# Four norms joined tile by tile with the stages around them

## What is computed

```python
# first block, end of the mixer, experts, final norm
h = h + g1 * (merged @ w_out)                     # mixer's out projection
x = modulate(rmsnorm(h, norm_ffn), sh2, sc2)      # "ffn" norm
h = h + g2 * hier_moe(x)                          # routed experts, 2 picks per token
h = rmsnorm(h, norm_final)                        # first final norm
# second block
hn = rms_norm(h, g_mix)                           # "mix2" norm
# ... latent and dilated attention on hn @ w_in ...
h = h + mixed @ w_out                             # attention's out projection
h = h + peer_ffn(rms_norm(h, g_ffn))              # "ffn2" norm, memory stage
gate = sigmoid(rms_norm(h, g_ple) @ w_ple_gate)   # "ple" norm, gate projection
h = h + gate * (p @ w_ple_proj)
return rms_norm(h, g_final)                       # last norm
```

## Time and profile before

| | us |
|---|---|
| runs of the kernel before | 3147.31, 3138.82, 3145.73 |
| their median | 3145.73 |
| profiled execution | 3139.65 |
| its span, first to last instruction | 3137.8 |
| TensorE busy, share | 2779.3, 89% |
| VectorE busy, share | 1446.8, 46% |
| ScalarE busy, share | 534.6, 17% |
| GpSimd busy, share | 748.5, 24% |

### The profile page before, as it was taken

The page is one execution under the profiler, slowest core; times in us unless marked ns, Lnnn a source line. Parts: engine busy times, 40 slices in busy tenths (PEclk is TensorE's granted clock), DMA queues, the critical chain, the costliest instruction groups (busy, mean ns, idle before and its releaser), DMA issues. The chain is left out here.

```text
span 3137.8 us, 28344 instructions
## 1 busy us (share of the span) xinstructions
PE 2779.3 (89%) x10072; PEld 1566.3 (50%) x10072; DVE 1446.8 (46%) x2990; ACT 534.6 (17%) x1149; POOL 748.5 (24%) x620
## 2 busy tenths in 40 slices
PE   6999999999997699949889989999866789888877
PEld 3446534456444333324445578888755633333333
DVE  1135200112011322231057249888789977777762
ACT  2024200011001011130147121111122400000011
POOL 0000000000000122110000004456588556555630
PEclk9999998999997799979899999999988999999998
DMA  5101241520123699841300028999999689999981
GB/s 206 54 27 56 108 188 61 221 91 34 54 107 135 242 420 391 340 185 54 115 14 1 27 89 310 408 389 394 374 331 369 218 347 413 413 412 413 413 352 74
DMA packets 142432, 694.17 MB, mean 221 GB/s; under 512 B 20451, under 2 KB 21859, under 8 KB 110563
## 3 DMA queue, kind: packets, MB, share of 16 engines
q1 hardware_dynamic: 59716, 408.31, 33.1%
q0 software_dynamic: 81792, 281.07, 23.1%
q10 hardware_dynamic: 800, 3.15, 0.3%
HBM read 701.89 MB, written 48.23 MB: 239 GB/s over the span
## 5 line engine op out<-in xcount | busy, mean ns | idle before, releaser
L2237 POOL DMA_INDIRECT wring<-in_peer_u,pm_rows x256 | 368.5, 1440 | 736.4 <-DVEq L2530 536.8
L2349 PE MATMUL ps<-hT 128*128 128x512 f32 x1024 | 462.5, 604 | 65.7 <-DVE hT L2554 43.8
L422 PE MATMUL ps<-hT,wring 128*128 128x512 f32 (+2 forms) x1232 | 467.8, 541 | 13.5 <-DMA pm_iota<-in_row_numbers 3.5
L422 PE MATMUL ps<-hT,pm_coef_table 128*128 128x256 f32 x2048 | 451.2, 382 | 0.0
L422 PEld LDWEIGHTS ps<-hT,pm_coef_table 128*128 128x128 f32 x2048 | 392.3, 193 | 53.6
L2560 DVE SCALAR_TENSOR_TENSOR h_tok<-wring,pm_coef,h_tok 128x1024 f32<-128x1024 f32 x256 | 325.0, 1282 | 119.0 <-DMA wring<-in_peer_v,pm_rows 117.4
L2237 POOL DMA_INDIRECT wring<-in_peer_v,pm_rows x256 | 314.0, 1227 | 248.6 <-DVE h_tok L2560 209.8
L2349 PEld LDWEIGHTS ps<-hT 128*128 128x128 f32 x1024 | 189.8, 191 | 337.8 <-issue 232.8
L422 PEld LDWEIGHTS ps<-hT,wring 128*128 128x128 f32 (+1 forms) x1232 | 233.6, 191 | 241.3 <-issue 232.8
L2439 DVE CUSTOM_DVE_ANT_0 wring<-wring,pm_coef_table 128x1024 f32<-128x1024 f32 x256 | 306.0, 1232 | 71.8 <-DMA wring<-in_peer_u,pm_rows 66.6
L1454 POOL COPY ex_idx<-row_token 128x1 uint32 (+1 forms) x24 | 4.5, 186 | 1174.4 <-PEq L1586 1043.7
(11 more groups left out here) (416 smaller groups left out, 2759.6 us busy)
## 6 DMA issues: line engine op xcount, KB each, us to landing
ex_gu<-in_experts SPq DMA_DIRECT2D x32, 2048.0 KB
pm_coef_table<-in_peer_uT SPq DMA_DIRECT2D x64, 1024.0 KB
hT<-in_peer_v SPq DMA_DIRECT2D x64, 1024.0 KB
ex_dn<-in_experts SPq DMA_DIRECT2D x48, 1024.0 KB
wring<-in_w_in SPq DMA_DIRECT2D x21, 2048.0 KB, 8.6
wring<-in_experts SPq DMA_DIRECT2D x16, 2048.0 KB
ada_w<-in_w_ada SPq DMA_DIRECT2D x12, 2048.0 KB
g_dram_out<-pm_coef_table SPq DMA_DIRECT2D x64, 256.0 KB
```

The costliest lines, as they stand in the source:

```text
L422: mm = env.nc.tensor.matmul(out, w[:, k, lo:hi], rhs(k), start=(k == 0), stop=(k == KD - 1))
L2237: nc.gpsimd.indirect_dma_start(ring[n % RING], None, dram[name], bass.IndirectOffsetOnAxis(ap=rows[:, t, j:j + 1], axis=0)).then_inc(got[n ...
L2349: mm = nc.tensor.matmul(env.ps[:, OUT[k], :], W[n % 2][:, at:at + P], vr[p % 2][:, m % 2 * D + k % 2 * WBLK:m % 2 * D + (k % 2 + 1) * WBLK ...
```

## The change

A class `TileNorm` does the same norm for one token tile at a time: ScalarE squares tile t and takes its root, VectorE takes the reciprocal and scales the tile, TensorE transposes its eight 128x128 blocks into two banks, ScalarE evicts the first bank and VectorE the second, in four instructions each of 128x128. It is woven into its neighbours:

- The mixer's out projection takes the token tile outermost and both weight blocks within, and its tiles go tile 0, tile 1, transposes of 0, tile 2, transposes of 1, and so on; the store of xn goes tile by tile.
- The expert sum has the first final norm and the "mix2" norm behind it in one stage. ScalarE evicts four of the eight p @ w_ple_proj products ahead of its first scaling, and the other four later. The row of gains is one more load in this stage, and the stage waits for its stores.
- The attention's out projection takes the token tile outermost, with the transposes of tile i-1 behind the products of tile i. Both weight blocks are now free only when the last tile is reached.
- The "ple" norm, the gate projection and the last norm are one stage: transposes of tiles 0 and 1, gate products of tile 0, transposes of 2 and 3, the other gate products; each tile is normed by row and stored as soon as its sum is complete. Square roots and sigmoids alternate on ScalarE.

Six stages with their barriers are gone: four `stage_norm` and two `stage_rownorm`.

```diff
+class TileNorm:
+    def rows_on_scalar(self, act, t):
+        nc.scalar.activation(self.xn[:, t, :], self.env.h[:, t, :], ACT.Square, accum_out=self.ss[:, t, :]).then_inc(self.sq_done, 1)
+        act.wait_ge(self.sq_done, self.sq0 + t + 1)
+        nc.scalar.activation(self.rs[:, t, :], self.ss[:, t, :], ACT.Sqrt, scale=1.0 / D,
+                             bias=self.env.eps[:, 0:1]).then_inc(self.rms_done, 1)
+    def rows_on_vector(self, v, t):
+        v.wait_ge(self.rms_done, self.r0 + t + 1)
+        nc.vector.reciprocal(self.ss[:, t, :], self.rs[:, t, :]).then_inc(self.inv_done, 1)
+        v.wait_ge(self.inv_done, self.i0 + t + 1)
+        nc.vector.tensor_scalar(self.xn[:, t, :], self.env.h[:, t, :], self.ss[:, t, :], None, ALU.mult).then_inc(self.done, 1)
+    def on_tensor(self, pe, t):
+        pe.wait_ge(self.done, self.done0 + t + 1)
+        for half, tl in enumerate(self.tiles[t]):
+            bank_ready(env, pe, tl)
+            for j in range(4):
+                mm = nc.tensor.transpose(env.ps[:, tl[0], j * P:(j + 1) * P],
+                                         self.xn[:, t, (4 * half + j) * P:(4 * half + j + 1) * P], env.ident[:])
+            mm.then_inc(env.bank_full[tl[0]], 1)
+    def columns_on_scalar(self, act, t):
+        product_done(env, act, tl)
+        for j in range(4):
...
+    def columns_on_vector(self, v, t):
+        product_done(env, v, tl)
+        for j in range(4, KD):
...
@@ stage_out
-                for half in range(2):
-                    cs = slice(half * WBLK, (half + 1) * WBLK)
-                    for i, t in enumerate(tl[half]):
+                for i in range(NT):
+                    for half, t in enumerate(tl[i]):
+                        cs = slice(half * WBLK, (half + 1) * WBLK)
...
+                    if i >= 1:
+                        N.columns_on_vector(v, i - 1)
+                    N.rows_on_vector(v, i)
+                N.columns_on_vector(v, NT - 1)
...
+                tile(0)
+                for i in range(NT):
+                    if i + 1 < NT:
+                        tile(i + 1)
+                    N.on_tensor(pe, i)
@@ stage_expert_sum, scalar
+                projected(0, 4)
+                first(0)
+                first(1)
+                squares(0)
+                first(2)
+                squares(1)
+                rows(0)
+                first(3)
+                squares(2)
+                rows(1)
+                projected(4, 8)
+                N.columns_on_scalar(act, 0)
+                squares(3)
+                rows(2)
+                N.columns_on_scalar(act, 1)
+                rows(3)
+                N.columns_on_scalar(act, 2)
+                N.columns_on_scalar(act, 3)
@@ stage_expert_sum, vector
+                v.wait_ge(row_in, run16 + 16)
+                summed(0)
+                summed(1)
+                normed(0)
+                summed(2)
+                normed(1)
+                N.rows_on_vector(v, 0)
+                summed(3)
+                normed(2)
+                N.rows_on_vector(v, 1)
+                N.columns_on_vector(v, 0)
+                normed(3)
+                N.rows_on_vector(v, 2)
+                N.columns_on_vector(v, 1)
+                N.rows_on_vector(v, 3)
+                N.columns_on_vector(v, 2)
+                N.columns_on_vector(v, 3)
@@ stage_attention_out, tensor
-                for half in range(2):
-                    w = block_view(env, pe, bl[half])
-                    for i in range(NT):
-                        ts = slice(i * P, (i + 1) * P)
-                        for kind, t in enumerate(tl[half][i]):
+                for i in range(NT):
+                    ts = slice(i * P, (i + 1) * P)
+                    for half in range(2):
+                        w = block_view(env, pe, bl[half])
+                        for kind, t in enumerate(tl[i][half]):
...
+                    if i >= 1:
+                        N.on_tensor(pe, i - 1)
+                N.on_tensor(pe, NT - 1)
@@ stage_embedding
-                nc.sync.dma_start(proj[:], dram["p_dram"].rearrange("(t p) d -> p t d", p=P)).then_inc(in_s, 16)
                 load_blocks(env, sp)
+                nc.sync.dma_start(proj[:], dram["p_dram"].rearrange("(t p) d -> p t d", p=P)).then_inc(in_s, 16)
+                nc.sync.dma_start(row[:], dram["g_final_row"].broadcast_to([P, D])).then_inc(row_in, 16)
+                for t in range(NT):
+                    sp.wait_ge(done, t + 1)
+                    nc.sync.dma_start(dram["out"][t * P:(t + 1) * P, :], env.h[:, t, :]).then_inc(out_s, 16)
...
+                N.on_tensor(pe, 0)
+                N.on_tensor(pe, 1)
+                gates(0)
+                N.on_tensor(pe, 2)
+                N.on_tensor(pe, 3)
+                for t in range(1, NT):
+                    gates(t)
```

More of the change, by code:

```diff
@@ L1656, in _, with stage_expert_sum @@
                 product(LAST - 1, 1)
-def stage_expert_sum(env, E):
+def stage_expert_sum(env, E, row_name, gain):
     nc, dram = env.nc, env.dram
     got = [env.again(f"gathered{t}", 16 * PICKS)[0] for t in range(NT)]
-    first_s = env.sem("es_first")
-    p_t = env.tiles(2 * NT)
+    first_s, sum_s, sq_s, rms_s, inv_s, fin_s = (env.sem("es_" + n) for n in ("first", "sum", "sq", "rms", "inv", "fin"))
     p_in, pin0 = env.again("proj_in", 32)
+    row_in, run16 = env.again("row_in", 16)
     p_out, out0 = env.again("row_out", 16 * NT)
@@ L1670, in stage_expert_sum @@
         y = T("y", [P, NT, PICKS, D])
-        pT, wp, proj = T("pT", [P, PLE // P, S]), T("wp", [P, PLE // P, D]), E.proj
+        pT, wp, proj = T("pT", [P, PLE // P, S]), T("wp", [P, PLE // P, D]), T("proj", [P, NT, D])
+        row, ss, rs = T("row", [P, D]), T("ss", [P, NT]), T("rs", [P, NT])
+        p_t = env.tiles(2 * NT)
+        N = TileNorm(env, st, "mix2", gain)
+        for t in range(NT):
+            N.tile()
         with nc.Block() as block:
@@ L2023, in _, with stage_attention_out @@
                         mm.then_inc(env.bank_full[pv[u][0]], 1)
[L2026 removed]
+def stage_attention_out(env, mixT, sq, gain):
     nc = env.nc
[L2029 to L2036 removed]
     rms_s, inv_s, sum_s = (env.sem("ao_" + n) for n in ("rms", "inv", "sum"))
@@ L2040, in stage_attention_out @@
         rs, iv = (st.enter_context(nc.sbuf_tensor("ao_" + n, [P, NT, 2], F32)) for n in ("rs", "iv"))
+        N = TileNorm(env, st, "ffn2", gain)
+        tl, t_ss = [], None
+        for i in range(NT):
+            tl.append([])
+            for half in range(2):
+                tl[i].append(env.tiles(2))
+                if t_ss is None:
+                    t_ss = env.tile()
+            if i >= 1:
+                N.tile()
+        N.tile()
+        bl = [env.take_block(t[-1]) for t in tl[-1]]
         with nc.Block() as block:
```

241 lines of the change are left out of this document (171 added, 70 removed).

## The result

The changed kernel takes 3113.14 (median of four runs, 3109.1 to 3119.28) against 3143.85 for the kernel before (four runs, 3138.82 to 3147.31): a ratio of 0.991, 95% interval 0.989 to 0.993. Timed again beside experiment e9 it was 3115.31 against 3143.60, a ratio of 0.991 (0.989 to 0.992). So it is 28 to 31 us faster; the forecast was 3116, with 26.3 for the change. The profiled execution has a span of 3114.0 against 3137.8.

What follows compares the result with a forecast made beforehand. TensorE was busy 89% of the span, so its standstill and lower clock at four seams could be won: 8.7 - 0.2 + 4.9 + 12.9 = 26.3 (mixer, expert sum, attention, last stretch). From 3142.7 that gave 3116, range 3102 to 3130.

Steps and rivals of the forecast that it cites:

- Mixer: Mixer's out projection and FFN norm: no stall at second weight block, norms of tiles 0 to 2 hidden; 8.7 won.
- T3: The last token tile's eight transposes; at the mixer's seam 1.2, plus half a microsecond for the lower clock.
- Attention: Attention's out projection and FFN norm: memory stage opens 6.6 sooner, 4.9 won after the clock's charge.
- The charge of 1.7 for the clock: Behind the attention's out projection: TensorE starts at the lower clock after 4 us idle, 1.7 lost.
- Last stretch: Final gate projection, PLE norm and final norm: gate matmuls start 7.3 sooner, shorter tail; 12.9 won.
- the expert sum: Expert sum with two norms behind it: 1.5 won, less 1.7 for the clock, so -0.2.
- the ledger of 7.8 a tile: VectorE's work per token tile in the expert sum's stage: 7.8, or 31.3 for four.
- The clock's charge of 1.7: At the projection behind the expert sum: short transpose bursts with waits leave TensorE cold; 1.7 lost (0 to 1.9).
- (a): Expert sum and attention seams give less through engine hops and late query weights: 19.3, or 3123; chance 0.20.
- (b): At the expert-sum and attention seams the clock stays high over the gaps: 3.4 more, 3113; chance 0.12.
- (c): Transposes between matmuls drop the clock in a whole out or gate projection: slower, 3171; chance 0.03.
- (d): Memory stage and experts take up earlier gains; only the last stretch counts, half lost to DMA: 3136; chance 0.07.

Runs made afterwards that it cites:

- e9: Changed kernel with the edits of e6, e7 and e8 together; 3105.54, ratio to the kernel before 0.988.
- e10: Changed kernel without any edit, timed over five rounds beside e9; 3115.31.
- e1: Kernel before with only the mixer's out projection and the FFN norm joined; 3135.80.
- e2: Kernel before with only the expert sum, first final norm and second block's first norm joined; 3135.46.
- e4: Kernel before with only the last norm of tokens, gate projection and final norm joined; 3133.76.
- e5: Changed kernel without any edit, one more profiled execution; 3113.06.
- e8: Changed kernel plus idle transposes of the identity behind the attention's last transposes and at the memory stage's and last stretch's openings; 3112.42.
- e11: Changed kernel with the mixer's norms and transposes moved behind all its out-projection products, still in one stage; 3127.56.
- e6: Changed kernel with two gathered tiles scaled ahead of the projection's evictions in the expert sum, evictions split two and six; 3105.92.
- e7: Changed kernel with tile 1's transposes moved behind tile 3's products in both out projections; 3117.58.
- e12: e11 with all four tiles' squares, roots and scalings ahead of the evictions of transposed columns; 3116.90.
- e3: Kernel before with only the attention's out projection and the norm behind it joined; 3132.24.

## Why the prediction was right, and where it was not

**What held.** That the seams are what can be won, and that a gain passes on whole: stretches between the seams keep their lengths to within about 2 (router and experts 360.0 to 362.1, projection and attention 332.1 to 333.7 where TensorE starts it warm), but for the memory stage, which scatters by 10 in unchanged code. **Mixer:** no stall at the second weight block, norms of tiles 0 to 2 hidden; 8.0 against 8.7. Some 0.3 of the difference is T3, which runs wholly cold (1.97, after 3.13 of rest; with the half microsecond taken off I had 1.7), and 0.3 is e10's cold start in the mean. ScalarE's four evictions with gain and shift, 1.49 to 1.51 in place of 1.2, are off the path: they end at 991.27, VectorE's at 991.98. Without shift they are 1.12 to 1.18. **Attention:** the memory stage opens 6.9 sooner by the means, counted from the first out product (6.6 forecast), its first matmul comes 2.52 later, the second block of query weights is in time. The charge of 1.7 for the clock was 2.2 in the profile and 1.4 between the means. But e1 and e2, whose seam there is as before, also started their queries partly cold (0.71 and 0.73 over the first 3 us), while the profiled execution before and e4 did not. So before the change two of four paid, behind the merged seam all eight without fillers, and the net is 5.5 against 4.9. **Last stretch:** weights 7.97 after the opening (forecast 8), end 74.30 after it (forecast 74.7). Over five executions with a warm start (the changed kernel, e5, e8, e10, e11) the mean is 74.55, a gain of 12.8 against 12.9 from the stages' mean before of 87.4; over five with a cold start (e4, e6, e7, e9, e12) it is 76.54. I had taken TensorE for warm there after two tiles of transposes, and that holds in half of the executions: a term of 1 that was missing.

**The step that was mis-sized** is the expert sum: forecast -0.2, measured 3.5 at the seam and 2.9 with what the projection gives back. Its two terms in the prediction were the ledger of 7.8 a tile and the clock. The ledger for four tiles was 31.3 and the list takes 29.1, because the pitches are shorter than I had added up. An instruction that does not wait for the one in front of it starts some 0.1 before that one ends (the second tile's sum at 1374.12, the addition before it ends at 1374.20; in the kernel before each waited, 1370.40 and 1370.43). A sum takes 3.72 (3.84 forecast), reciprocal and final scaling 1.39 (1.6), the second norm's 0.86 (1.0), four evictions 1.04 (1.4, the price of VectorE's evictions with shift and a hop). The start of the chain, 17.9 after the opening by the forecast, is 17.2 to 20.3, set by the landing of es_wp. The clock's charge of 1.7 was met in three of ten executions, all three of them with an edit of mine (e6, e7, e9); in the other seven the projection began at 1.00. In the changed kernel the last two tiles' transposes ran as one group (3.73 at 1394.60) with 1.64 of rest behind them; I had them as two bursts with 3 or more between.

The Trainium skill (TensorE: Matmul & The Clock Gate, "HAM oscillation — how this bites in real kernels") has short bursts parted by waits begin cold each time. The trace agrees at the queries (3.9 to 4.6 of rest, 0.50 in eight of eight). The projection is no such case: its rest of 1.64 behind one group of transposes is shorter than the waits of the page's example, and it began at 1.00 in seven of ten. The rest alone does not decide it, though: where the seam is as before, with 3.4 to 3.6 of rest behind 32 transposes, the queries began at 1.00 in two of four.

**The rivals.** (a), two tight seams that give less, did not come: VectorE's list in the expert sum shows no wait on ScalarE, and the query weights are in time. (b), a clock that stays high over the gaps, holds at one of the two seams. (c), transposes between matmuls that drop the clock: the 32 matmuls between two groups of transposes took 13.90 in the mixer's projection (changed kernel and e10), where at half the clock they would take about twice that (an estimate). (d) is refuted by e1 to e3, which gain with the last stretch as before. **The total.** 3113.1 and 3115.3 against 3116, inside the range. The kernel before stood at 3143.9 and 3143.6, where I had put the sum on 3142.7; the expert sum gave 3 more than forecast, and a cold gate in half of the executions and the mixer's seam took some 1.8 back. So the total is closer than its parts: the expert sum was put 3.7 too low and the attention seam 0.6, the mixer's seam and the last stretch 1.8 too high together, and 1.1 more goes back in between. That these cancel in part is luck.

## What to carry to other kernels

A norm between two stages costs its full chain of engines once per stage; woven in tile by tile it costs one tile's chain, but only where other work as long as that chain stands beside each tile: without it, an in-order list that puts a tile's last step ahead of the next tile's first makes the joined stage slower than two stages with a barrier. Price such a stage by walking the list of its busiest engine, with the pitches from one start to the next that a trace shows, for instructions that wait for each other and for those that don't, and look at what stands ahead of the chain's first instruction on the engine that feeds it (four evictions there cost more here than any hop). Count a cold start of TensorE as a cost that comes in some executions and not in others, and compare stretches over several profiles before believing 2 us.

## What the hardware showed that I had not expected

- **The same code starts warm or cold.** The granted clock of the first matmuls behind a rest differs between executions of the same stretch of code: mixer's out projection 27.70 or 29.40 for 64 matmuls (the changed kernel and e10, the same kernel), gate 13.97 or 15.80 for 32, the queries behind the seam as before 3.73 or 5.41 to their first eviction. Each costs 1.7 to 1.8. The Trainium skill (TensorE: Matmul & The Clock Gate, "What's actually happening") says that the number of slow matmuls at a kernel's start varies from run to run; these rows show the like in the middle of one.
- **A table load costs its 1.28 and no more.** The accumulator read ends at 3107.86, the load starts at 3107.88, the root at 3109.17. The Trainium skill (ScalarE: Activation LUTs, "What ACT_TABLE_LOAD costs") adds a drain of about 1.38 to each switch, which no row here shows. Two switches per tile, hidden beside the gate's products, cost nothing.
- **An eviction of 128x128 is cheap to repeat.** Four take 1.12 on VectorE and 1.15 on ScalarE with a gain, 1.37 and 1.50 with gain and shift.
